# Solving block 2's triangular systems in 64x64 blocks, two heads to a group, with the decay taken from cumulative gates

## The reference, cut to what matters

```python
def hybrid_mixer(h, positions, ...):
    out_a = sliding_window_attention(aq, ak, av, sinks)     # 8 query heads, window 128
    o_b = hgrn2_chunked(bq, log_f, bv)                      # 4 heads of 64
    o_c = gated_delta_chunked(cq, ck, cv, beta, g)          # 4 heads of 64

def gated_delta_chunked(q, k, v, beta, g):
    G = jnp.cumsum(gc, axis=-1)
    L = jnp.exp(jnp.where(incl, G[..., :, None] - G[..., None, :], -jnp.inf))
    kb = kc * bc[..., None]
    A = jnp.where(strict, jnp.einsum('bnhtd,bnhsd->bnhts', kb, kc) * L, 0.0)
    T = lax.linalg.triangular_solve(eye + A, ..., lower=True, unit_diagonal=True)
    U = T @ (vc * bc[..., None])
    W = T @ (kb * jnp.exp(G)[..., None])
    qk = jnp.where(incl, jnp.einsum('bnhtd,bnhsd->bnhts', qc, kc) * L, 0.0)
    def step(state, inp):
        v_new = u - w @ state
        o = qd @ state + qkc @ v_new
        state = gl[..., None, None] * state + jnp.swapaxes(kd, -1, -2) @ v_new
```

## Time and profile before

| | us |
|---|---|
| median of 3 executions | 3743.59 |
| lowest and highest | 3733.34, 3747.10 |
| span of the profiled execution | 3742.8 |
| the mixer's stage of layer 0, first matmul to the end of its last work | 2342.2 to 2541.0 |
| the mixer's stage of layer 1, first matmul to the end of its last work | 3125.3 to 3322.4 |

### The profile page before, as it was taken

One profiled execution on the slowest core, in us unless ns is written; L12 is line 12 of the kernel. 1 busy time (PEld: TensorE's weight loads), 2 busy tenths in 40 slices (PEclk: granted clock), 3 DMA queues, 4 the chain that ended last, 5 costly groups with the idle time before them and its releaser, 6 DMA issues. The chain is left out here.

```text
span 3742.8 us, 41241 instructions
## 1 busy us (share of the span) xinstructions
PE 3612.7 (97%) x16434; PEld 2831.1 (76%) x16434; DVE 2194.7 (59%) x2932; ACT 1294.1 (35%) x1898; POOL 743.3 (20%) x448
## 2 busy tenths in 40 slices
PE   8999998999999999989999999999999999999999
PEld 6888744888878888537888867786888767867887
DVE  6655557765575556567655676566444656645444
ACT  3223235422242223345322453445222344443221
POOL 3432002343213430011444022220000021300000
PEclk9999999999999999999999999799999998989999
DMA  5433211444334342203434221002322220012222
GB/s 178 141 130 123 96 39 45 144 136 138 116 108 139 127 141 96 74 24 116 147 126 144 93 76 56 1 13 76 104 94 98 84 73 18 13 57 86 99 98 85
DMA packets 97950, 351.09 MB, mean 94 GB/s; under 512 B 11808, under 2 KB 12064, under 8 KB 96864
## 3 DMA queue, kind: packets, MB, share of 16 engines
q1 hardware_dynamic: 97760, 348.46, 28.0%
HBM read 345.93 MB, written 2.42 MB: 93 GB/s over the span
## 5 line engine op out<-in xcount | busy, mean ns | idle before, releaser
L412 ACT ACTIVATE w_hi<-raw 128x1024 fp32r<-128x1024 f32 (+2 forms) x538 | 556.1, 1037 | 1802.7 <-PE ps L336 1717.9
L334 PE MATMUL ps<-xs_hi,w_hi 128*128 128x512 f32 x2304 | 908.4, 394 | 2.5 <-DVE arena L1299 2.5
L336 PE MATMUL ps<-xs_hi,w_lo 128*128 128x512 f32 x2304 | 900.6, 391 | 0.0
L335 PE MATMUL ps<-xs_lo,w_hi 128*128 128x512 f32 x2304 | 900.0, 391 | 0.0
L422 DVE TENSOR_TENSOR w_lo<-raw,w_hi 128x1024 fp32r<-128x1024 f32 (+2 forms) x538 | 671.3, 1249 | 148.9 <-ACT w_hi L412 148.3
L334 PEld LDWEIGHTS ps<-xs_hi,w_hi 128*128 128x128 f32 x2304 | 434.7, 189 | 104.5 <-issue 14.8
L335 PEld LDWEIGHTS ps<-xs_lo,w_hi 128*128 128x128 f32 x2304 | 435.0, 189 | 93.7 <-issue 3.6
L336 PEld LDWEIGHTS ps<-xs_hi,w_lo 128*128 128x128 f32 x2304 | 434.5, 189 | 91.3
L334 PE MATMUL ps<-hd_hi,w_hi 128*128 128x512 f32 x1280 | 500.2, 391 | 1.6 <-DVE hd_lo L1036 1.6
L336 PE MATMUL ps<-hd_hi,w_lo 128*128 128x512 f32 x1280 | 498.1, 389 | 0.0
L335 PE MATMUL ps<-hd_lo,w_hi 128*128 128x512 f32 x1280 | 497.9, 389 | 0.0
(11 more groups left out here) (476 smaller groups left out, 4524.7 us busy)
## 6 DMA issues: line engine op xcount, KB each, us to landing
raw<-in_ffn_gu SPq DMA_DIRECT2D x264, 512.0 KB, 3.8
arena<-in_ada SPq DMA_DIRECT2D x64, 768.0 KB, 5.8
raw<-in_ffn_dn SPq DMA_DIRECT2D x96, 448.0 KB, 3.3
raw<-in_in_t SPq DMA_DIRECT2D x60, 512.0 KB, 3.6
raw<-in_ffn_dn SPq DMA_DIRECT2D x48, 512.0 KB, 3.5
raw<-in_out SPq DMA_DIRECT2D x32, 512.0 KB, 3.6
raw<-in_pleg SPq DMA_DIRECT2D x16, 512.0 KB, 3.6
raw<-in_in_r SPq DMA_DIRECT2D x8, 512.0 KB, 3.5
```

What stands on the lines that cost most here:

```text
L334: T.matmul(bank, lhs_hi(k), rhs_hi(k), start=(first and k == 0), stop=False)
L335: T.matmul(bank, lhs_hi(k), rhs_lo(k), start=False, stop=False)
L336: mm = T.matmul(bank, lhs_lo(k), rhs_hi(k), start=False, stop=(last and k == kt - 1))
L412: A.activation(self.hi[:, n % HL, 0:size], raw[:, n % RAW, 0:size], ACT.Copy).then_inc(self.high_done, 1)
```

## The change

1. Preparation. PE spreads `rowG`, the cumulative gates, in place of `rowg`, the gates. DVE subtracts the token's own cumulative gate (a column of `dcols`) and takes the minimum with 0 in one `tensor_scalar` per chunk, 4 per head, in place of a multiplication and a scan per head. ACT takes the exponential in place (`gm`). The multiplication by `upto` is gone from DVE; POOL applies `upto` to `qkT` alone, one head at a time. `kb` gets its factor -1 in the same instruction that forms it, so that later subtractions become copies.
2. The solve. The levels 0 to 5 work on the diagonal 64x64 blocks. The four heads form two groups (c = 0, 1) of two heads. Of each head's chunk one diagonal block lies on partitions 0 to 63 and the other on 64 to 127, in `Tc` and `Tn` (now `[H, ST, 64]`). A phase is 16 matmuls of 64x64 per group, 32 in all, alternating between the two halves of the partitions, in contraction and in output. A level has three phases, each a turn of its own: product with `Tn`, product with `Tc`, and transposition (a matmul with the identity). DVE updates by a copy under the mask `blocks` from PSUM, 512 columns for each group, and POOL masks nothing more. Level 6 joins the two blocks of a chunk with two phases of 16 matmuls and a copy into the corner of `Tt`; POOL copies the diagonal blocks of `Tc` into `Tt`. The solve has 18 pieces, one a turn, in the turns 6 to 23; `TWICE` is gone.
3. U and W come in turn 24, the recurrence in the turns 25 to 32. W's matmuls run over the heads inside the chunk.
4. HGRN. `hgrn_pe` waits for `inv_rows_ready` before its first products. The output products yield after each head (four turns), and the norm's squares follow each group's copy. `scale_output` comes two pieces earlier.

The local attention is the same. The core of the diff:

```diff
-    TWICE = range(5, 11)
...
-            if turn in TWICE:
-                next(first)
...
-        AT, qkT, Tn, Tt = [b_space.get(H, ST, P) for _ in range(4)]
+        AT, qkT, Tt = [b_space.get(H, ST, P) for _ in range(3)]
+        Tn, Tc = [b_space.get(H, ST, HD) for _ in range(2)]
...
+                pe.wait_ge(inv_rows_ready, 1)
...
-                        T.matmul(ps[6 + e][:, :], pick(4, 2 * c + e), rowg[R4, :], start=True, stop=True).then_inc(spread, 1)
+                        T.matmul(ps[6 + e][:, :], pick(4, 2 * c + e), rowG[R4, :], start=True, stop=True).then_inc(spread, 1)
...
+                for v in range(NL):
+                    if v:
+                        for c in range(2):
+                            pe.wait_ge(n_updated, 2 * v + c - 1)
+                            for h in range(2):
+                                for j in range(ST):
+                                    for e, r in enumerate(heads_of):
+                                        if v < NL - 1:
+                                            mm = T.matmul(block(ps[4 + c], e, h, j), AT[r, 2 * c + h, j, 64 * e:64 * e + 64],
+                                                          Tn[r, 2 * c + h, j, :], start=True, stop=True)
...
+                            mm.then_inc(xt_done, 1)
+                        yield
...
+                            mm.then_inc(z_done, 1)
+                        yield
+                    if v < NL - 1:
+                        for c in range(2):
+                            pe.wait_ge(t_updated, 2 * v + c + 1)
...
+                                        mm = T.matmul(block(ps[4 + c], e, h, j), Tc[r, 2 * c + h, j, :],
+                                                      C("ident")[r, 64 * e:64 * e + 64], start=True, stop=True)
+                            mm.then_inc(tt_done, 1)
+                        yield
+                pe.wait_ge(t_updated, 2 * NL)
+                pe.wait_ge(prepared, 7)
...
-                        order.done(V.tensor_tensor(gx, ps[6 + e][:, :], C("strict4"), ALU.mult))
-                        V.tensor_tensor_scan(gx, C("strict4"), gx, 0.0, ALU.mult, ALU.add).then_inc(scan_ready, 1)
+                        for j in range(ST):
+                            q = slice(j * P, (j + 1) * P)
+                            ins = V.tensor_scalar(gm[:, e, q], ps[6 + e][:, q], dcols[:, j, 32 + g:33 + g], 0.0,
+                                                  ALU.subtract, ALU.min)
...
-                        order.done(V.tensor_tensor(chunks(Lx), chunks(Lx), C("upto").unsqueeze(1).to_broadcast([P, ST, P]), ALU.mult))
...
+                            if v < NL - 1:
+                                V.copy_predicated(blocks_of(Tc, c), masks[:, v, :].unsqueeze(1).to_broadcast([P, 2 * ST, HD]),
+                                                  in_bank(ps[6 + c][:, :])).then_inc(t_updated, 1)
...
-                for i, (v, hd) in enumerate(turns):
...
-                    G.tensor_tensor(low_[:, i % 2, :, :], AT[:, hd, :, :],
-                                    C("levels", None, v * P, (v + 1) * P).unsqueeze(1).to_broadcast([P, ST, P]), ALU.mult) \
-                     .then_inc(low_ready, 1)
+                for c in range(2):
+                    pool.wait_ge(t_updated, 2 * (NL - 2) + c + 1)
+                    for e, r in enumerate(heads_of):
+                        G.tensor_copy(blocks_of(Tt, c)[r, :, 64 * e:64 * e + 64], blocks_of(Tc, c)[r, :, :]).then_inc(prepared, 1)
+                        pool.wait_ge(prepared, 4 + 2 * c + e)
```

More of the change, by code:

```diff
@@ L66, in constant_columns @@
     out["levels"] = np.concatenate(lev, 1)
+    out["blocks"] = np.concatenate([np.concatenate([a[0:HD, 0:HD], a[HD:P, HD:P]], 0) for a in lev[:-1]], 1)
     q, k = i[:, None], np.arange(2 * P)[None, :]
@@ L107 @@
 BLOCK1 = ("rot_mla", "from", "dft_c", "dft_s", "dft_n")
-BLOCK2 = ("rot_win", "strict4", "levels", "window", "restart")
+BLOCK2 = ("rot_win", "blocks", "levels", "window", "restart")
 def pack(columns):
@@ L2476, in mixer2 @@
         steps = [(v, c) for v in range(NL) for c in range(2)]
-        turns = [(v, hd) for v in range(NL) for hd in range(H)]
-        NS = len(turns)
+        blocks_of = lambda a, c: a[:, 2 * c:2 * c + 2, :, :].rearrange("p h j k -> p (h j) k")
+        in_bank = lambda bank: bank.rearrange("p (m k) -> p m k", k=HD)
         sk = c2["sinks"][0]
@@ L2734, in hgrn_act @@
                     A.activation(hg[:, c, :], ps[c][:, :], ACT.Copy).then_inc(o_copied, 1)
-                act.wait_ge(o_copied, 2)
-                for c in range(2):
+                    act.wait_ge(o_copied, c + 1)
                     hg_norm.act_square(act, c)
-                yield
+                    yield
                 hg_norm.act_root(act)
@@ L2807, in hgrn_dve @@
                     yield
-                yield
-                yield
-                yield
+                for _ in range(6):
+                    yield
                 hg_norm.dve_invert(dve, slice(0, S // 2))
@@ L2900, in delta_pe @@
                 mm.then_inc(u_done, 1)
-                for hd in range(H):
-                    for j in range(ST):
+                for j in range(ST):
+                    for hd in range(H):
                         mm = T.matmul(ps[6 + hd // 2][64 * (hd % 2):64 * (hd % 2) + 64, j * P:(j + 1) * P],
@@ L2946, in delta_act @@
                         act.wait_ge(scan_ready, 2 * c + e + 1)
[L2947 to L2949 removed]
+                        A.activation(gm[:, e, :], gm[:, e, :], ACT.Exp).then_inc(l_ready, 1)
                     yield
                     yield
[L2952 to L2963 removed]
+                for v in range(NL):
+                    if v:
+                        for c in range(2):
+                            act.wait_ge(xt_done, 2 * v + c - 1)
+                            r = slice(0, P) if v < NL - 1 else heads_of[1]
+                            A.activation(flat(Lm)[r, c * S:(c + 1) * S], ps[4 + c][r, :], ACT.Copy).then_inc(xt_ready, 1)
+                        yield
+                        yield
+                    if v < NL - 1:
+                        for c in range(2):
+                            act.wait_ge(tt_done, 2 * v + c + 1)
+                            A.activation(blocks_of(Tn, c), in_bank(ps[4 + c][:, :]), ACT.Copy).then_inc(n_updated, 1)
+                        yield
                 act.wait_ge(u_done, 1)
@@ new lines, in delta_dve @@
+                masks = C("blocks").bitcast(I32).rearrange("p (v k) -> p v k", k=HD)
+                for v in range(NL):
+                    if v:
+                        yield
+                        for c in range(2):
+                            dve.wait_ge(z_done, 2 * v + c - 1)
+                            if v < NL - 1:
+                                V.copy_predicated(blocks_of(Tc, c), masks[:, v, :].unsqueeze(1).to_broadcast([P, 2 * ST, HD]),
+                                                  in_bank(ps[6 + c][:, :])).then_inc(t_updated, 1)
+                            else:
+                                top_ = heads_of[0]
+                                V.tensor_copy(blocks_of(Tt, c)[top_, :, HD:P], in_bank(ps[6 + c][top_, :])).then_inc(t_updated, 1)
+                        yield
+                    else:
+                        dve.wait_ge(prepared, 2)
+                        for c in range(2):
+                            dve.wait_ge(head_ready, 4 * c + 3)
+                            for e, r in enumerate(heads_of):
+                                ins = V.copy_predicated(blocks_of(Tc, c)[r, :, :], masks[r, v, :].unsqueeze(1).to_broadcast([HD, 2 * ST, HD]),
+                                                        blocks_of(AT, c)[r, :, 64 * e:64 * e + 64])
+                            ins.then_inc(t_updated, 1)
+                    if v < NL - 1:
+                        yield
```

133 lines of the change are left out of this document (46 added, 87 removed).

## The result

| | before | after |
|---|---|---|
| median, us | 3744.64 (4 executions, 3733.34 to 3747.10) | 3707.28 (4 executions, 3695.63 to 3712.29) |
| span of the profiled execution, us | 3742.8 | 3709.6 |

The ratio is 0.9897, 95% interval 0.9872 to 0.9921. The change makes the kernel 37 us faster by the medians; the forecast was 3695, 48 us faster, and its range (3677 to 3733) holds the result. The four executions of the changed kernel lie 16.7 us apart (before: 13.8), and they go with the mean granted clock: 3695.6 us at 0.977, 3703.2 at 0.974, 3711.3 and 3712.3 at 0.971.

A forecast was written before the change was run, and what follows sets the result against it. PE was taken to bound most of mixer2, with a chain in its tail. Gains of 12.5, 4.3 and 13.9 made 31 us per layer, less 7 for the clock: 24, 48 in all, giving 3695 us; range 3677 to 3733.

The forecast's parts named there:

- Price of the new matmul: Solve: an alternating 64x64 matmul costs 0.072 us, a phase of 32 takes 2.3; other end 0.129 and 4.1.
- Turns 6 to 14: Up to HGRN's first level product: 56.7 us before, 44.2 after, a gain of 12.5 per layer.
- The waits put in: Turns 6 to 14: PE waits 1.3 us for DVE's first masked copies, 2.7 for DVE's long piece ahead of the levels.
- Preparation: Turns 0 to 5: DVE's saved scans stay hidden behind PE, gain 0; at most 1 us if PE waits.
- The 14 level products: HGRN's first to last level product: 47.3 us before, 43.0 after; gain 4.3, or loss 1.0 with slow U and W.
- POOL's copies: Copies of Tc into Tt before U: covered by three turns (8 us); uncovered they would cost 5 us.
- the half phases: Level 6's phases of 16 matmuls: priced at 1.15 us; their two turns at 2.7 each, set by DVE.
- The tail: Last level product to the stage's end: 45.7 us before, 31.8 after, gain 13.9 as U and W leave it.
- Sum: Per layer: 31 us at the full clock, less 5 for slow U and W and 2 for dips, 24.
- Hand-overs: Rival, chance 0.16: waits on ACT or DVE add 0.5 us to each of turns 6 to 23; 3714 us.
- No overlap: Rival, chance 0.16: the solve's small matmuls cost 0.129 us each, a phase 4.1; 3731 to 3738 us.
- The slow clock: Rival, chance 0.08: clock falls to 1.2 GHz for the solve; loss of 17 us per layer, 3778 us.
- the prediction's sign: Solve: a granted clock of 0.9 or more was expected; below 0.75 the slow-clock rival would hold.

The follow-up runs named there:

- e6: e1 with U, W and the recurrence held back by four turns, until the last level product is out: 3707.7 us, ratio 0.9899 to the kernel before.
- e7: e1 with the old preparation's cost on DVE (multiplication and scan per head, mask by upto; output not the reference's): 3692.5 us, ratio 0.9858.
- e5: Changed kernel with level 6's other quadrant filled by unused matmuls and the four copies into Tt moved to ACT, placed earlier than in e3: 3684.1 us.
- e10: e5 with unused 64x64 matmuls filling PE's waits before level 3's product with Tc and HGRN's first level product: 3677.6 us, ratio 0.9812.
- e1: Changed kernel with level 6's other quadrant given the same number of matmuls, whose results nobody reads: 3689.5 us, ratio 0.9859 to the kernel before.
- e12: The changed kernel measured again, unaltered, beside e10 on the same chip: 3705.7 us, ratio 0.9894 to the kernel before.
- e4: Changed kernel with each solve phase running the first quadrant's 16 matmuls, then the second's, in place of alternating: 3714.0 us, ratio 0.9925.
- e3: Changed kernel with level 6 filled and the four copies into Tt on ACT, two in level 6's second phase, two in U's turn: 3701.8 us.
- e11: e5 with the six matmuls that spread beta and gates from 4 rows made over 128 rows with other data (output not the reference's): 3659.1 us.
- e9: e3 with 34 unused 64x64 matmuls filling PE's wait ahead of U: 3687.1 us, ratio 0.9839 to the kernel before.

## Why the prediction was nearly right, and where it was not

- **Price of the new matmul, 0.072 us.** Measured 0.063, alternating. The row taken (four matmuls in alternating output halves) was the right neighbour; the other end, 0.129, is close to the price of a single quadrant (0.126).
- **Turns 6 to 14, gain 12.5.** Measured 13.1 in both layers for the preparation and these turns together, 0.9 of it in the preparation of layer 0; the first level product came at 92.6 where 93 was said. The waits put in (1.3 and 2.7) were 1.8 for DVE's masked copies and 1.83 and 1.14 ahead of the levels, and PE waited 1.38 for ACT's part of the attention besides; the cheaper phases paid for the difference. That it came so close is in part luck: with the half clock for 33 us ahead of the first level product it is 92.6, but e6, with the same matmuls up to there, has 87.5 in layer 0 (20 us of it) and 98.4 in layer 1 (44).
- **Preparation, 0.** Right (e7).
- **The 14 level products, 43.0 to 48.4.** This is the term that was mis-sized: 53.0 and 57.9. At the full clock the sum was good: 41.9 in e5's layer 0 and in e10. Terms in it cancelled, though: U and W were priced at 0.129 a matmul, 4.1 us, and take 5.6 (e1), the three turns of the recurrence were put at 9.2 and take 6.8, and the seven full turns at 23.3 and take 21.4. The 11.1 us between 41.9 and layer 0's 53.0 are 1.2 of waiting (1.69 against 0.46, POOL's copies slowing DVE), 2.0 in the first turn at the low clock, and 7.9 for the half clock from 2464 to 2482, in level 6, two of HGRN's products, U and W. The sum had 5 for U and W and 2 for dips. In layer 1 the same fall lasts 37 us, over the recurrence as well, and costs 12.8 of the 57.9 and 3.1 of the tail; the wait and the first turn take 3.1 there, as in layer 0.
- **The two steps behind that.** POOL's copies were said to be covered, and in time they were; that they slow DVE beside them was not counted, though the earlier trace rows had shown just that for the masks. And the half phases were priced at half of a full one, while their matmuls are all in one quadrant and cost the same; with HGRN's product their turns take 3.05 at the full clock where the sum had 2.7.
- **The tail, gain 13.9.** 15.3 in layer 0, 12.1 in layer 1. U and W off the chain (e6).
- **Sum.** 24 per layer were forecast; 22.8 and 14.6 came. Layer 0 was nearly right; what is missing is layer 1's fall, twice as long as layer 0's, where the sum had the same 7 us for both. In the second profile of the changed kernel (e12) it lasted 24 us there, and the levels took 53.8.
- **The rivals.** Hand-overs didn't bind: the full turns take 3.05 us, with one wait of 0.40 among them. No overlap is refuted (e4). The slow clock held in part: over the turns 6 to 27 the granted clock was 0.88 in layer 0 and 0.82 in layer 1, so about a quarter and a third of that time went at the half clock, and not the two thirds at which it would have decided. In the solve alone it was 0.91 in layer 0, as the prediction's sign wanted.

What stays open: how long a fall lasts. The same kernel gave 3689 and 3715 (e3), the changed one 3696 to 3715 over eight executions. Where full phases ran, it was over in 3 to 14 us in all profiles. Where level 6 in one quadrant, U and W ran it held for 17 to 38, where U and W ran behind full phases for 10 to 27 (10 and 27 in the two layers of e3, with the same work), and for 7 in the kernel before; no run varied that alone. Nor does every wait bring a fall: with level 6 filled, 1.7 us ahead of it did so in three of eight layers. Open is also whether the spreading over 128 rows helps in a valid form, with the 4 rows padded by zeros; no run has it, and zeros may not count as other data does.

## What to carry to other kernels

Price a change at both clocks, and look in every stretch for what went with the low one in these runs: a wait of PE (1.7 to 2.5 us) with work other than full phases behind it, and the matmuls of 4 rows. A fall of the clock cost 2 to 5 us where full phases followed and 8 to 16 where level 6 in one quadrant, U and W did. Small matmuls are worth packing by alternating quadrants, filling the idle quadrant of level 6 with work that nobody needs cost nothing, and a copy that is in time can still cost something on POOL if DVE is the engine beside it.

## What the runs showed of the hardware

- 64x64 matmuls of 64 float32 columns: 0.063 us each in two alternating quadrants that write to one PSUM bank, 0.104 in runs of eight per quadrant, 0.126 in one quadrant.
- At the half clock U's 16 matmuls (128 rows, 128 outputs, 64 columns) take 7.09 us, at the full clock 3.79.
- DVE's 256-column operation takes 0.41 us alone and 0.83 beside a POOL copy of 64 partitions by 512.
- Matmuls of 4 rows by 512 columns, six of them in 30 us, go with a granted clock of 0.5 for 20 to 34 us although PE is busy; over 128 rows and with other data the same stretch runs at 1.00, and 25 us of the program go away (e11 against e5).
- PE kept busy through a wait of 2.45 us with matmuls that nobody reads keeps the clock at 1.00 behind it (e9).
